# Three layers of modulation vectors, and two parts of the first one's, as dot products along the free axis on VectorE

## The chip, the cores and the metric

One core of one Trainium2 chip. The metric is the device time in microseconds; the kernel before was run 3 times on the chip and executed once more under the profiler. Matmuls are in float32 or float32r.

## The reference

Four diffusion-transformer layers on 256 latent and 256 context tokens of width 1024, followed by a second block (pooling, gated linear attention, a mixture of experts). What the change touches is how each layer's modulation vectors are made:

```python
silu_c, silu_cc = silu(c), silu(c_ctx)                 # two vectors of 1024
for i in range(4):
    sh_a, sc_a, g_a, sh_m, sc_m, g_m = split(silu_c @ mod_w[i] + mod_b[i], 6)   # mod_w[i]: 1024 x 6144
    # the same with silu_cc for the context stream where it is still used
    h = rms_norm(x, norm_mix_g[i]) * (1 + sc_a) + sh_a
    x = x + g_a * mixer(h)          # Fourier, differential attention, latent attention, Fourier
    h = rms_norm(x, norm_mlp_g[i]) * (1 + sc_m) + sh_m
    x = x + g_m * square(relu(h @ w1)) @ w2
```

So `mod_w` is 4 matrices of 25 MB, each multiplied with one or two vectors.

## The kernel before

Activations lie feature-major: feature `128*m + p` of tile `m` on partition `p`, tokens along the free axis, latent (columns 0 to 255) beside context. Every weight matrix is read in panels of 1024 rows by 128 columns. A panel is split into two float32r parts: ScalarE copies `w_hi` (`split_hi`), VectorE subtracts to get `w_lo` (`split_lo_at`), and TensorE makes three products per 128 rows (`split_product`). There is a ring of 4 split panels, and a panel is split 3 ahead of its use (`AHEAD`). An MLP is 4 blocks; a block is 16 steps `j`, one panel each: 8 of the first matrix (then relu and square), 8 of the second (then `add_gated`, which needs the gate vector). The order on each engine is written out by hand; SyncE issues all loads of 1 MB units in one queue, and waits in it for the buffer of each.

The modulation vectors are made in two ways:

- Layer 0: 24 units (`mod_unit`) of 128 rows by 2048 columns, 8 for each third of the 6144 columns. A unit is 4 float32 matmuls side by side in the array, with the two silu vectors as the weights' columns (32 wide, zero padded). ScalarE copies the sum to SBUF, `turn_first` transposes it, and `first_read` on VectorE adds the bias. The last third (shift, scale and gate; the scale is its middle part) is made while the Fourier mixer's last projection runs: units 0 and 1 behind panel 1, 2 and 3 behind panel 2, then one behind each of the panels 3 to 6; its transposes stand behind panel 7.
- Layers 1 to 3: 96 loads of 128 rows by 1536 columns. VectorE multiplies each with the scalar of its partition and adds it to `mod_acc` (`mod_fold`), inside the MLPs of the layers 0 to 2. After 8 loads `sum_mod` adds over the partitions with 8 matmuls on TensorE (`mod_acc` against a column of ones), ScalarE copies, `turn_mod` transposes, and `mod_read` copies to `mod`. There are 9 such groups, 4 in `mlp0`, 4 in `mlp1`, 1 in `mlp2`.

Between two stages of the first layer (`boundary`), the projection's panels 4 to 7 are made for the latent half first and then for the context half (`half_outputs`), so that the norm of the latent half can start early. In it TensorE stands at `half_sum` (the sum of squares over the partitions, behind 4 of the 8 products of the first context tile) until VectorE has added the square of the last latent tile (`add_square`).

Of the kernel before, what the change touches and what calls it, by code (L numbers as in the profile page):

```python
# [380 lines left out]
MOD_RING = 4  # L381
MOD_COLS = 6 * D // BLOCKS
MOD_UNITS = KT
MOD_PART = MOD_COLS // 4
MOD_STEPS = [1, 2, 4, 5, 7, 8, 10, 11]
MOD_SUM_AT = 13
FIRST_GROUPS = 3
FIRST_COLS = 6 * D // FIRST_GROUPS
FIRST_PART = FIRST_COLS // 4
FIRST_RING = 3  # L390
FIRST_UNITS = FIRST_GROUPS * MOD_UNITS
ROWS_AFTER = {1: range(0, 3), 2: range(3, 6), 3: range(6, 9), 4: range(9, 12), 5: range(12, 14), 6: range(14, 16)}
SCALED_AHEAD = [("scale", 0), ("scale", 1), ("sum", 0), ("scale", 2), ("sum", 1), ("scale", 3), ("sum", 2), ("sum", 3)]
THIRD_GROUP_AT = {1: [0, 1], 2: [2, 3], 3: [4], 4: [5], 5: [6], 6: [7]}


MOD_TO = {}
MOD_FOLDS = {}


def place_mods():


    n = 0
    for b in range(BLOCKS):
        MOD_TO[FIRST_GROUPS + b] = [(1, b, 0, 2)]
        MOD_FOLDS[0, b] = [(MOD_STEPS[u], n + u, 1, b, u, (0, 1)) for u in range(MOD_UNITS)]
        n += MOD_UNITS
    for b in range(2):
        MOD_TO[FIRST_GROUPS + BLOCKS + b] = [(2, b, 0, 2)]  # L410
        MOD_FOLDS[1, b] = [(MOD_STEPS[u], n + u, 2, b, u, (0, 1)) for u in range(MOD_UNITS)]
        n += MOD_UNITS
    for b in range(2, BLOCKS):
        MOD_TO[FIRST_GROUPS + BLOCKS + b] = [(2, b, 0, 1), (3, b - 2, 1, 1)]
        MOD_FOLDS[1, b] = [(MOD_STEPS[u], n + 2 * u + i, 2 + i, b - 2 * i, u, (i,))
                           for u in range(MOD_UNITS) for i in range(2)]
        n += 2 * MOD_UNITS
    MOD_TO[FIRST_GROUPS + 2 * BLOCKS] = [(3, 2, 0, 1), (3, 3, 1, 1)]
    for b in range(BLOCKS):
        MOD_FOLDS[2, b] = [((1, 4, 8, 11)[q], n + q, 3, 2 + q % 2, 2 * b + q // 2, (q % 2,)) for q in range(4)]  # L420
        n += 4
    MOD_FOLDS.update({(3, b): [] for b in range(BLOCKS)})


place_mods()
MOD_READ = {(1, 0): 5, (1, 1): 7, (2, 0): 9, (2, 1): 11, (3, 0): 11, (3, 1): 12}


def mod_group(layer, b):


    if layer == 2:
        return FIRST_GROUPS + 2 * BLOCKS if isinstance(b, int) and b == BLOCKS - 1 else None
    return FIRST_GROUPS + BLOCKS * layer + b if layer < 2 and isinstance(b, int) else None
# [3 lines left out]
def build_program(nc, a, out):  # L438
# [8 lines left out]
    with ctx:  # L447
# [46 lines left out]
        pick = sb("pick", [P, 2, 32])  # L494
# [4 lines left out]
        mod_raw = [sb(f"mod_raw{r}", [P, MOD_COLS]) for r in range(MOD_RING)]  # L499
        mod_rows = sb("mod_rows", [P, MOD_PART], over=at["vec_rows"])  # L500
        first_raw = [sb(f"first_raw{r}", [P, FIRST_COLS], over=work + r * 4 * FIRST_COLS) for r in range(FIRST_RING)]
        assert FIRST_RING * FIRST_COLS <= MOD_RING * MOD_COLS
        mod_acc = sb("mod_acc", [P, 2, MOD_COLS])
# [5 lines left out]
        base = at["mod_acc"]  # L509
# [8 lines left out]
        first_rows = sb("first_rows", [P, FIRST_PART])  # L518
        assert base <= at["mod_acc"] + 2 * MOD_COLS * 4, base
# [96 lines left out]
        assert base <= at["mod_acc"] + 2 * MOD_COLS * 4, base  # L616
# [46 lines left out]
        mod_ps = psum[4]  # L663
        pv_ps = psum[4]
# [48 lines left out]
        mod_w = a["mod_w"].rearrange("l (k p) (b c) -> l b k p c", p=P, b=BLOCKS)  # L713
        first_w = a["mod_w"][0].rearrange("(k p) (b c) -> b k p c", p=P, b=FIRST_GROUPS)
# [25 lines left out]
        def _(sp):  # L740
# [21 lines left out]
            def load_mod(n, layer, block, u, i=None):  # L762

                freed = n - MOD_RING + 1
                if freed > 0 or i is not None:
                    sp.wait_ge(s("mod_folded"), later(freed, i, MOD_UNITS))
                else:
                    sp.wait_ge(s("first_used"), FIRST_UNITS)
                sp.dma_start(mod_raw[n % MOD_RING][:, :], mod_w[layer, block, u]).then_inc(s(f"mod_in{n % MOD_RING}"), 16)

            def load_mlp(layer, region_free=None):
# [8 lines left out]
                def mods(n, b):  # L780
                    _, n, of, block, u, _ = MOD_FOLDS[layer, b][n]
                    load_mod(n, of, block, u)

                def block(b, text):
                    for x in text.split():
                        what, n = x[0], int(x[1:])
                        if what == "w":
                            weights(n, b)
                        elif isinstance(b, int):
                            mods(n, b)  # L790
                        else:
                            load_mod(n, 1, b, n, b)

                eight = "w0 m0 m1 w1 m2 w2 m3 w3 w4 w5 m4 m5 w6 m6 w7 m7"
                sixteen = "w0 m0 m1 w1 w2 m2 m3 w3 w4 w5 m4 m5 w6 m6 m7 w7 m8 m9 m10 m11 m12 m13 m14 m15"
                if layer == 0:
                    block(0, eight)
                    with sp.Fori(1, BLOCKS) as b:
                        block(b, eight)
                elif layer == 1:  # L800
                    block(0, "w0 w1 w2 w3")
                    region_free()
                    block(0, "m0 m1 m2 m3 w4 w5 m4 m5 w6 m6 w7 m7")
                    block(1, eight)
                    block(2, sixteen)
                    block(3, sixteen)
                elif layer == 2:
                    block(0, "w0 w1 w2 w3")
                    region_free()
                    block(0, "m0 m1 m2 m3 w4 w5 w6 w7")  # L810
                    for b in range(1, BLOCKS):
                        block(b, "m0 m1 w0 m2 w1 w2 m3 w3 w4 w5 w6 w7")
                else:
                    with sp.Fori(0, BLOCKS) as b:
                        block(b, "w0 w1 w2 w3 w4 w5 w6 w7")

            mod_b = a["mod_b"].rearrange("l (r c) -> (l r) c", c=P)
# [13 lines left out]
            def load_first(units):  # L831
                for n in units:
                    if n >= FIRST_RING:
                        sp.wait_ge(s("first_used"), n - FIRST_RING + 1)
                    sp.dma_start(first_raw[n % FIRST_RING][:, :],
                                 first_w[n // MOD_UNITS, n % MOD_UNITS]).then_inc(s(f"first_in{n % FIRST_RING}"), 16)

# [8 lines left out]
            load_first(range(FIRST_RING, MOD_UNITS - 3))  # L846
# [3 lines left out]
            load_first(range(MOD_UNITS - 3, MOD_UNITS))  # L850
            four_w = a["fourier_w"][0].rearrange("(k p) (u c) -> u p k c", p=P, c=2 * P)
            load_first(range(MOD_UNITS, 2 * MOD_UNITS))
# [5 lines left out]
            load_first(range(2 * MOD_UNITS, FIRST_UNITS))  # L858
# [3 lines left out]
            for h in range(HEADS // 2):  # L862
# [3 lines left out]
                if h == 0:  # L866
                    sp.wait_ge(s("mod_read"), FIRST_GROUPS + BLOCKS)
# [11 lines left out]
            sp.wait_ge(s("mod_read"), FIRST_GROUPS + 2 * BLOCKS)  # L879
# [30 lines left out]
            sp.wait_ge(s("mod_summed"), 2 * BLOCKS + 1)  # L910
# [69 lines left out]
        def _(pool):  # L980
# [5 lines left out]
            pool.memset(pick[:, :, :], 0.0).then_inc(s("pick"), 1)  # L986
            pool.wait_ge(s("pick"), 1)
            for st in range(2):
                pool.memset(pick[:, st, st:st + 1], 1.0).then_inc(s("pick"), 1)
# [47 lines left out]
        def _(act):  # L1037
# [108 lines left out]
            def boundary(n0, x0, name, layer, group=None):  # L1146
# [1699 lines left out]
        def _(dve):  # L2846
# [53 lines left out]
            def boundary(n0, t0, x0, name, layer, gate, before=0, group=None):  # L2900
# [32 lines left out]
                if group:  # L2933
                    mod_read(group, MOD_TO[group])
# [1110 lines left out]
```

## Time and profile before

| | |
|---|---|
| runs | 2028.79, 2032.46, 2033.71 us (median 2032.46) |
| the profiled execution | span 2028.9 us; the page gives no other time of it |
| granted TensorE clock, mean | 0.984 |
| TensorE busy | 96% |
| VectorE busy | 73% |
| ScalarE busy | 50% |
| DMA | 343.51 MB, mean 169 GB/s |

The span is from the first to the last instruction. In the page's lines "L1842" is a line of the kernel, "out<-in" are buffers with their numbers left out, and "x" counts instructions. Matmuls overlap, so the distance between two starts says what one costs, and not its duration.

### The profile page before, as it was taken

What the parts mean: (1) busy time and instruction counts of PE and PEld (TensorE: products, weight loads), DVE (VectorE), ACT (ScalarE), POOL (GpSimd) and SP (SyncE); (2) the same over time, 40 slices, a digit from 0 to 9 for tenths busy, and PEclk for the clock granted to TensorE, in tenths of its full rate; (3) what the DMA queues carried; (4) which work ended last, traced back from release to release, by engine and by line L of the source; (5) the groups of instructions that cost most, each with busy time, mean ns of one, the idle gap of its engine ahead of it and who ended that gap; (6) DMA issues with size and microseconds to landing.
All of it is one profiled execution on the core that took longest, in us unless ns stands there. A gap on an engine that the chain in (4) does not pass through costs nothing.

```text
span 2028.9 us, 31376 instructions
## 1 busy us (share of the span) xinstructions
PE 1947.6 (96%) x11840; PEld 1693.3 (83%) x11840; DVE 1479.8 (73%) x2298; ACT 1023.4 (50%) x1730; POOL 21.7 (1%) x43
## 2 busy tenths in 40 slices
PE   6999999999999999999999787999999999999998
PEld 4688888889787888888888667999999999997886
DVE  3569576687667758685858588788887667776796
ACT  5353323235666656232333577555555456655685
POOL 0200000000000000000000100000000000000000
PEclk9999999999999999999999899999999999999999
DMA  7866464541211234545765311577645555417795
GB/s 288 326 206 211 139 211 136 169 158 48 84 63 63 68 119 132 193 151 167 263 237 166 83 54 46 188 259 265 217 125 182 187 165 168 131 60 232 261 355 196
DMA packets 257044, 343.51 MB, mean 169 GB/s; under 512 B 24487, under 2 KB 235266, under 8 KB 253842
## 3 DMA queue, kind: packets, MB, share of 16 engines
q1 hardware_dynamic: 256914, 341.74, 50.7%
q8 instruction: 85, 1.39, 0.3%
q14 instruction: 45, 0.37, 0.1%
HBM read 340.67 MB, written 1.05 MB: 168 GB/s over the span
## 4 chain that ended last, share of the span: by engine, by line
PE 79%; DVE 8%; ACT 6%; issue 4%; DMA 1%; SPq 0%; DVEq 0%; ACTq 0%
PE bank L1842 24%; PE bank L1843 23%; PE bank L1844 23%; PE bank L2694 2%; PE bank L2684 1%; ACT p_raw L1396 1%; DVE w_lo L2849 1%; ACT p_raw L1384 1%; DVE p_all L3358 1%; PE bank L1894 1%; ACT w_hi L1048 1%; PE bank L1913 1%; ACT mp_raw L1564 1%; ACT norm L1141 1%; DVE neg_max L3367 1%
## 5 line engine op out<-in xcount | busy, mean ns | idle before, releaser
L2849 DVE TENSOR_TENSOR w_lo<-w_raw,w_hi 128x1024 fp32r<-128x1024 f32 x449 | 546.0, 1222 | 60.6 <-ACT w_hi L1048 31.6
L1048 ACT ACTIVATE w_hi<-w_raw 128x1024 fp32r<-128x1024 f32 x350 | 368.0, 1053 | 387.6 <-PE bank L1844 379.2
L1842 PE MATMUL bank<-h_hi,w_hi 128*128 128x512 f32 (+3 forms) x1360 | 467.2, 344 | 10.2 <-DVE h_lo L2886 6.0
L1843 PE MATMUL bank<-h_lo,w_hi 128*128 128x512 f32 (+3 forms) x1360 | 460.3, 338 | 0.0
L1844 PE MATMUL bank<-h_hi,w_lo 128*128 128x512 f32 (+3 forms) x1360 | 459.7, 338 | 0.0
L1842 PE MATMUL bank<-g_hi,w_hi 128*128 128x256 f32 (+1 forms) x1216 | 404.0, 332 | 6.8 <-DVE g_lo L3412 3.6
L1843 PE MATMUL bank<-g_lo,w_hi 128*128 128x256 f32 (+1 forms) x1216 | 400.0, 329 | 0.0
L1844 PE MATMUL bank<-g_hi,w_lo 128*128 128x256 f32 (+1 forms) x1216 | 399.8, 329 | 0.0
L1842 PEld LDWEIGHTS bank<-h_hi,w_hi 128*128 128x128 f32 x1360 | 257.7, 189 | 49.7 <-issue 12.8
L1844 PEld LDWEIGHTS bank<-h_hi,w_lo 128*128 128x128 f32 x1360 | 257.7, 189 | 27.6
L1843 PEld LDWEIGHTS bank<-h_lo,w_hi 128*128 128x128 f32 x1360 | 257.9, 190 | 26.4 <-issue 0.3
L1842 PEld LDWEIGHTS bank<-g_hi,w_hi 128*128 128x128 f32 x1216 | 232.2, 191 | 34.9 <-DVE g_lo L3412 4.5
L1844 PEld LDWEIGHTS bank<-g_hi,w_lo 128*128 128x128 f32 x1216 | 232.1, 191 | 20.5
L1843 PEld LDWEIGHTS bank<-g_lo,w_hi 128*128 128x128 f32 x1216 | 232.3, 191 | 19.4
L3004 DVE SCALAR_TENSOR_TENSOR mod_acc<-mod_raw,silu_c,mod_acc 128x1536 f32<-128x1536 f32 x126 | 224.8, 1812 | 1.5
L3073 DVE SCALAR_TENSOR_TENSOR x<-bank,mod,x 128x256 f32<-128x256 f32 x192 | 87.4, 480 | 114.4 <-PE bank L1844 113.6
L1301 ACT ACTIVATE norm<-bank 128x512 f32<-128x512 f32 x64 | 38.2, 597 | 189.4 <-PE bank L1844 189.4
L3220 DVE TENSOR_TENSOR norm<-norm 128x512 f32<-128x512 f32 (+1 forms) x128 | 70.9, 554 | 72.0 <-ACT norm L1301 67.4
L1739 ACT ACTIVATE w_hi<-w_raw 128x1024 fp32r<-128x1024 f32 x99 | 104.1, 1060 | 35.0 <-PE bank L1844 23.6
L3223 DVE TENSOR_TENSOR g_lo<-norm,g_hi 128x512 fp32r<-128x512 f32 (+1 forms) x128 | 71.6, 559 | 13.3
L1842 PE MATMUL bank<-u_hi,w_hi 128*128 128x258 f32 x256 | 72.9, 285 | 0.0
L1843 PE MATMUL bank<-u_lo,w_hi 128*128 128x258 f32 x256 | 72.4, 283 | 0.0
(539 smaller groups left out, 2805.0 us busy)
## 6 DMA issues: line engine op xcount, KB each, us to landing
w_raw<-in_mlp_w SPq DMA_DIRECT2D x128, 1024.0 KB, 5.6
mod_raw<-in_mod_w SPq DMA_DIRECT2D x96, 768.0 KB, 4.7
first_raw<-in_mod_w SPq DMA_DIRECT2D x24, 1024.0 KB, 5.1
w_raw<-in_w_expert_gate SPq DMA_DIRECT2D x34, 512.0 KB, 4.8
w_raw<-in_w_expert_up SPq DMA_DIRECT2D x34, 512.0 KB, 6.1
w_raw<-in_w_expert_down SPq DMA_DIRECT2D x17, 1024.0 KB, 5.8
w_raw<-in_diff_w_qkv SPq DMA_DIRECT2D x12, 1024.0 KB, 5.1
w_raw<-in_fourier_w SPq DMA_DIRECT2D x8, 1024.0 KB, 7.6
```

What stands on the lines that cost most here:

```text
L1048: act.activation(split_panel(W_hi[n % RING], n), raw_panel(n), ACT.Copy).then_inc(s("w_hi"), 1)
L1301: act.activation(relu[j % 2][:, 0:n_cols], bank[(t0 + j) % BANKS][:, 0:n_cols], ACT.Relu).then_inc(s("relu"), 1)
L1739: act.activation(W_hi[(p0 + n) % RING][:, :], raw_panel(p0 + n), ACT.Copy).then_inc(s("w_hi"), 1)
L1842: pe.matmul(dst, w_hi, r_hi, start=start, stop=False)
L1843: pe.matmul(dst, w_hi, r_lo, start=False, stop=False)
L1844: return pe.matmul(dst, w_lo, r_hi, start=False, stop=stop)
L2694: ins = pe.matmul(slot_out[half][:, :], e[x % 2][:, k, 0:P], v[:, w], start=x % 4 == 0 and k == 0 and q == 0, stop=x % 4 == 3 and k == 1 a ...
L2849: dve.tensor_tensor(split_panel(W_lo[n % RING], n), raw_panel(n), split_panel(W_hi[n % RING], n).bitcast(F32), ALU.subtract).then_inc(s("p ...
L3004: ins = dve.scalar_tensor_tensor(acc, raw, c, acc, ALU.mult, ALU.add)
L3073: ins = dve.scalar_tensor_tensor(X[:, m, c], bank[t % BANKS][:, c], mod[layer][:, gate_at + m, st:st + 1], X[:, m, c], ALU.mult, ALU.add)
L3220: dve.tensor_tensor(squared, relu[j % 2][:, c], relu[j % 2][:, c], ALU.mult).then_inc(s("g_sq"), 1)
L3223: dve.tensor_tensor(G_lo[:, j, c], squared, G_hi[:, j, c].bitcast(F32), ALU.subtract).then_inc(s("g_lo"), 1)
```

## The change

The layer 0 matmuls keep two groups instead of three: shift and scale of the mixer, then its gate and the MLP's scale (2 rows of the 6, in two pieces). Everything else is made as follows. The host hands in `mod_w` transposed as well (`mod_t`, 6144 x 1024 per layer). A unit is now two tiles of 128 output features, each a row of 1024 inputs on its partition, 80 units of 1 MB in a ring of 3. The two silu vectors are spread over all partitions as `c_all`: TensorE transposes them once, they are written to a scratch tensor in HBM (`c_store`), and read back with a broadcast, once before `mlp0`, once in `mlp1` and once in `mlp2`. A fold is then one fused instruction, which multiplies the tile with `c_all`, sums along the free axis, starts from the bias and writes one column of `mod`. There are 240 folds; `MOD_STEPS` gives their places. 16 of them (the shift, 8 tiles for two streams) stand in the `boundary` before `mlp0`: 4 ahead of it and 2, 2, 2, 2, 1, 1, 1, 1 behind its tiles; ScalarE waits for them ahead of the latent half's norm. `pick`, `sum_mod`, `turn_mod`, `mod_read`, the third group of `mod_unit` and the ScalarE copies of these are gone.

```diff
-MOD_RING = 4
+MOD_RING = 3
+MOD_PAIR = 2
-FIRST_GROUPS = 3
+FIRST_GROUPS = 2
...
+    take("first", [(0, 4)])
+    take("four0", enumerate([2, 2, 2, 2, 1, 1, 1, 1]))
+    for b in range(BLOCKS - 1):
+        take(("mlp", 0, b), enumerate([2, 2, 1, 2, 2, 1, 2, 2] + [2] * KT))
+    take(("mlp", 0, BLOCKS - 1), enumerate([2] * KT + [2, 1, 2, 1]))
+    some = [2, 1] * 4
+    for b, counts in enumerate(([0, 0, 1, 1, 1, 1, 2, 2] + some, 2 * some, 2 * some, some + [2, 1, 2, 1, 2])):
+        take(("mlp", 1, b), enumerate(counts))
+    for b in range(BLOCKS - 1):
+        take(("mlp", 2, b), enumerate([0] * KT + [1] * KT))
...
+            def load_mod(n):
+                if n < MOD_RING:
+                    sp.wait_ge(s("first_used"), FIRST_UNITS)
+                else:
+                    sp.wait_ge(s("mod_folded"), sum(x[0] <= n - MOD_RING for x in MOD_OPS))
+                layer, t = MOD_UNITS[n]
+                sp.dma_start(mod_raw[n % MOD_RING][:, :, :],
+                             mod_w[layer, :, t:t + MOD_PAIR, :]).then_inc(s(f"mod_in{n % MOD_RING}"), 16)
+            def spread_c():
+                sp.dma_start(c_all[:, :, :].rearrange("p s c -> p (s c)"),
+                             c_store.rearrange("(o c) -> o c", o=1).to_broadcast([P, 2 * D])).then_inc(s("c_all"), 16)
...
                 root(name, LAT, 0)
+                if name == "mlp0":
+                    act.wait_ge(s("mod_folded"), folds_through(0, 4 * KT - 1))
...
-            def sum_mod(g, i=None):
-                pe.wait_ge(s("mod_read"), later(g, i, 1))
-                folded = {9: 64, 10: 80, 11: 96}.get(g, MOD_UNITS * (g - FIRST_GROUPS + 1))
-                pe.wait_ge(s("mod_folded"), later(folded, i, MOD_UNITS))
-                for row in range(2):
-                    for j in range(4):
-                        ins = pe.matmul(mod_ps[32 * j:32 * (j + 1), 0:MOD_PART], pick[:, row, :],
-                                        mod_acc[:, row, j * MOD_PART:(j + 1) * MOD_PART], start=(row == 0), stop=(row == 1))
...
-                    for u in THIRD_GROUP_AT.get(m, []):
-                        mod_unit(u, 2)
...
+            def mod_folds(stage, j):
+                for n, i, layer, t, st in MOD_STEPS.get((stage, j), []):
+                    dve.wait_ge(s(f"mod_in{n % MOD_RING}"), 16 * (n // MOD_RING + 1))
+                    dve.wait_ge(s("c_all"), 16 * (2 + (stage[1] if stage[0] == "mlp" else 0)))
+                    bias = vcol("mod_b_lo" if layer < 2 else "mod_b_hi", MOD_TILES * (layer % 2) + t)
+                    raw = mod_raw[n % MOD_RING][:, i, :]
+                    again = (n, i, layer, t, 1) in MOD_OPS and st == 0
+                    if again and folds_before(layer, t):
+                        dve.wait_ge(s("mod_folded"), folds_before(layer, t) - 1)
+                    dve.tensor_tensor_reduce(mod_prod[:, :] if again else raw, raw, c_all[:, st, :], 1.0, bias, ALU.mult,
+                                             ALU.add, mod[layer][:, t, st:st + 1]).then_inc(s("mod_folded"), 1)
...
                 first_read(1)
                 dve.wait_ge(s("mod_sum"), 2)
                 add_bias(0, 2)
+                mod_folds("first", 0)
                 boundary(p0, t + 4 * KT + 2, X_AT["four0"], "mlp0", 0, (0, 2 * KT))
```

`first_read` now copies and adds in two pieces and makes the scale in both of its calls (before: one piece, and no scale in the second). The VectorE and SyncE programs of `mlp0` are written out for each block instead of looped.

## Rows read from the trace of the kernel before

**Rows 1.** The page: span, busy time, and the chain that ended last.

```profile
span 2028.9 us, 31376 instructions
...
PE 1947.6 (96%) x11840; PEld 1693.3 (83%) x11840; DVE 1479.8 (73%) x2298; ACT 1023.4 (50%) x1730; POOL 21.7 (1%) x43
...
PE 79%; DVE 8%; ACT 6%; issue 4%; DMA 1%; SPq 0%; DVEq 0%; ACTq 0%
```

**Rows 2.** Busy windows: stretch, PE, PEld, DVE, ACT, POOL, clock, DMA share, GB/s.

```profile
148.00:235.50 87.50, 87.50 (x403) 71.55 (x403) 66.93 (x72) 30.48 (x39) 0.00 (x0) 1.00 0.56 181
...
81.44:119.70 38.26, 38.26 (x246) 27.84 (x245) 19.44 (x45) 8.77 (x14) 0.00 (x0) 1.00 0.64 228
```

**Rows 3.** The same view, a stretch of `mlp2`.

```profile
1360.00:1420.00 60.00, 60.00 (x500) 60.00 (x499) 50.64 (x74) 33.17 (x48) 0.00 (x0) 1.00 0.77 266
```

**Rows 4.** Groups by line, whole span: busy us, mean ns of one, idle before.

```profile
L3004 DVE SCALAR_TENSOR_TENSOR mod_acc<-mod_raw,silu_c,mod_acc 128x1536 f32<-128x1536 f32 x126 | 224.8, 1812 | 1.5
...
L3006 DVE TENSOR_SCALAR mod_acc<-mod_raw,silu_c 128x1536 f32<-128x1536 f32 x18 | 17.6, 1015 | 0.0
...
L1913 PE MATMUL bank<-mod_acc,pick 128*32 128x384 f32 x144 | 13.5, 492 | 0.0
```

**Rows 5.** TensorE's timeline at one group's sum and transposes: start, duration.

```profile
208.94 0.39 PE L1844 MATMUL bank<-g_hi,w_lo 128*128 128x512 f32 x1
209.25 1.50 PE L1913 MATMUL bank<-mod_acc,pick 128*32 128x384 f32 x16
210.68 0.50 PE L1842 MATMUL bank<-g_hi,w_hi 128*128 128x512 f32 x1
...
216.30 0.49 PE L1921 MATMUL bank<-ident,mod_rows 128*128 128x128 f32 x3
216.54 0.48 PE L1842 MATMUL bank<-g_hi,w_hi 128*128 128x512 f32 x1
```

**Rows 6.** TensorE's timeline at units of the third group.

```profile
86.50 0.39 PE L1844 MATMUL bank<-h_hi,w_lo 128*128 128x512 f32 x1
...
86.82 1.92 PE L1894 MATMUL bank<-first_raw,silu_c 128*32 128x512 f32 x16
...
88.67 0.51 PE L1842 MATMUL bank<-h_hi,w_hi 128*128 128x512 f32 x1
...
101.62 0.39 PE L1844 MATMUL bank<-h_hi,w_lo 128*128 128x512 f32 x1
...
102.94 0.39 PE L1842 MATMUL bank<-h_hi,w_hi 128*128 128x256 f32 x1
```

**Rows 7.** VectorE by line, 81.44 to 119.7 us: what ended its idle time.

```profile
L2914 DVE SCALAR_TENSOR_TENSOR x<-bank,mod,x 128x256 f32<-128x256 f32 x12 | 5.4, 480 | 18.5 <-PE bank L1844 18.5
```

**Rows 8.** Timeline: split of panel 3, last square added, TensorE's sum, last latent `h_lo`.

```profile
86.43 1.23 DVE L2849 TENSOR_TENSOR w_lo<-w_raw,w_hi 128x1024 fp32r<-128x1024 f32 x1
...
119.27 0.42 DVE L2869 TENSOR_TENSOR norm<-norm,norm 128x256 f32<-128x256 f32 x1 [0.15 <-ACT norm L1074]
...
119.97 0.60 PE L1954 MATMUL bank<-norm,ones 128*128 128x256 f32 x2
...
136.36 0.43 DVE L2886 TENSOR_TENSOR h_lo<-norm,h_hi 128x256 fp32r<-128x256 f32 x1 [0.52 <-ACT h_hi L1144]
```

**Rows 9.** TensorE alone in two windows: stretch, busy, granted clock, DMA share.

```profile
40.00:45.00 5.00, 1.51 (x12) 0.87 0.88 360
45.00:50.00 5.00, 4.59 (x20) 0.50 0.01 3
```

**Rows 10.** Timelines of VectorE and ScalarE: nearest operations to the new one.

```profile
22.07 2.48 DVE L3308 SCALAR_TENSOR_TENSOR rows_lo<-x_rows,o_inv,rows_hi 128x1024 fp32r<-128x1024 f32 x2 [1.29 <-ACT rows_hi L1371]
...
17.96 0.19 ACT L1360 ACTIVATION_READ_ACCUMULATOR row_squares<-x_rows 128x1 f32 x1
```

**Rows 11.** Loads: a kind with KB and median us to landing; SyncE's timeline.

```profile
mod_raw<-in_mod_w SPq DMA_DIRECT2D x96, 768.0 KB, 4.7
...
70.41 32.99 SPq L835 DMA_DIRECT2D first_raw<-in_mod_w  x8
```

More of the change, by code:

```diff
@@ L425 @@
-place_mods()
[L426 to L434, printed above, removed]
+    tiles = [(0, t) for part in ("shift_m", "gate_m") for t in range(LATER_FIRST[part], LATER_FIRST[part] + KT)]
+    tiles += [(layer, t) for layer in range(1, DEPTH) for t in range(MOD_TILES)]
@@ new lines, in place_mods, with take @@
+    for n in range(0, len(tiles), MOD_PAIR):
+        MOD_UNITS.append(tiles[n])
+        for i, (layer, t) in enumerate(tiles[n:n + MOD_PAIR]):
+            streams = 2 if layer < 2 or layer == 2 and t < 2 * KT else 1
+            MOD_OPS.extend((n // MOD_PAIR, i, layer, t, st) for st in range(streams))
+    at = 0
+    def take(stage, counts):
+        nonlocal at
+        for j, n in counts:
+            MOD_STEPS[stage, j] = MOD_OPS[at:at + n]
+            at += n
+    take("first", [(0, 4)])
@@ L438, in build_program, with folds_before, folds_through @@
+    assert at == len(MOD_OPS), (at, len(MOD_OPS))
+place_mods()
+def folds_before(layer, t):
+    return sum((x[2], x[3]) < (layer, t) for x in MOD_OPS)
+def folds_through(layer, t):
+    return folds_before(layer, t + 1)
 def build_program(nc, a, out):
@@ L857, in _ @@
                 load_unit(PLAN.at["four0"]["unit"] + u, [(whole, four_w[u])])
-            load_first(range(2 * MOD_UNITS, FIRST_UNITS))
+            sp.wait_ge(s("c_all"), 16)
+            spread_c()
+            for n in range(len(LATER_FIRST) * KT // MOD_PAIR // 2):
+                load_mod(next(mod_units))
             load_mlp(0)
@@ L2898, in apply, with boundary, folds @@
                     low_rows(name, KT - 1, c)
-            def boundary(n0, t0, x0, name, layer, gate, before=0, group=None):
+            def boundary(n0, t0, x0, name, layer, gate, before=0):
                 lat, con = slice(0, LAT), slice(LAT, TOK)
+                def folds(m):
+                    return {"mlp0": ("four0", m), "mix1": (("mlp", 0, BLOCKS - 1), KT + m)}.get(name, (None, m))
                 def gated(m, streams):
@@ L2931, in boundary @@
                     add_square(name, LAT, m - 1, 0)
+                    mod_folds(*folds(m))
                 add_square(name, LAT, KT - 1, 0)
-                if group:
-                    mod_read(group, MOD_TO[group])
-                if name == "mlp0":
-                    first_read(2)
                 if name == "mix1":
```

274 lines of the change are left out of this document (91 added, 183 removed).

## The prediction

> **What bounds the kernel now.** I read the page first [rows 1]: TensorE is busy for 96% of the span and holds 79% of the chain that ended last, VectorE 8%. The windows show what this means where the change works [rows 2]: in a block of `mlp0` TensorE never stops (87.50 of 87.50 us, clock 1.00) while VectorE has 66.93 us of work. In such a stretch a microsecond taken from TensorE's queue is a microsecond off the time, and VectorE's work costs nothing until it fills the stretch. So the first question is how much leaves TensorE, the second whether VectorE still fits, stage by stage. The stage where this is in doubt is the boundary before `mlp0`: from 81.44 to 119.70 us VectorE works 19.44 us and is idle for 18.8 [rows 2], almost all of it in waits for TensorE's tiles [rows 7], and that stretch ends in a meeting of the two: VectorE's last square ends at 119.69, TensorE's `half_sum` stands right behind it at 119.97 [rows 8]. The other stretches are seen in the groups by line and in the timelines.
>
> **What leaves TensorE.** Matmuls of a panel start 0.23 us apart. Behind the one at 208.94 the next would start at 209.17; with the sum between them it starts at 210.68, 1.51 later, and is itself 0.11 longer (0.50 for 0.39). The transposes cost 216.54 - 216.30 = 0.24, with 0.09 of the same [rows 5]. That is 1.95 us a group, and there are 9 groups (the 144 records of the sum are 9 times 8 matmuls of two passes each [rows 4]): **-17.6 us**, 8 of the 9 in places where TensorE never waits, the ninth in `mlp2`, which is the same [rows 3]. The third group of layer 0: two units together cost 88.67 - 86.73 = 1.94, one alone 102.94 - 101.85 = 1.09 [rows 6]; two pairs and four single ones are 8.2, with 0.1 behind each of the six and 0.4 for four transposes 9.2 us. These stand in the doubtful stretch.
>
> **What comes to VectorE.** 144 operations on 1536 columns go, 126 of 1.81 us and 18 of 1.01, 242 us in all [rows 4]. 240 fused operations on 1024 columns come. The trace shows none like it. The nearest is a three-operand one on 1024 columns with a pointer scalar: two in 2.48 us, so 1.20 from start to start [rows 10]. The new one also puts out a sum; on ScalarE such a read of the accumulator is 0.19 us [rows 10]. The cost lies between 1.15 (the 1.81 on 1536 columns scaled to 1024 gives 1.21, the last part overlapping) and 1.40 (1.20 plus the whole 0.19); I take **1.25**, near the three-operand row. Then 240 are 300 us, 58 more than before, spread over three MLPs.
>
> The Trainium skill (VectorE: DVE Perf Modes, "Two Vector instructions with no wait between them") says that an operation which also writes out its accumulator is two instructions. It gives no price; if that second one costs what ScalarE's does, the sum is that of the upper end, 1.40.
>
> **Do the MLP blocks hold it?** A block of `mlp0` has 66.93 of 87.50, of which 14 to 16 folds are 27.4; 39.5 is other work. With 30 folds of 1.25 it is 77, so TensorE stays the bound; the point from which VectorE decides is (87.5 - 39.5)/30 = 1.60 us a fold. In `mlp1` 20 to 24 folds of 1.25 stand in for 16 of 1.81: no more work than before. In `mlp2` VectorE has 50.64 of 60 [rows 3]; in a block of 46 us 8 folds (10.0) stand in for 4 (7.2), 90% in all; it fits with little room, and the panels split ahead take up a step that is too long. I cost all three at 0; the cover is VectorE's idle time, and below 1.60 us it lasts.
>
> Loads: a unit is issued when the unit three before it is folded. By the order in the diff, a unit in `mlp0` is issued 4 to 6 steps (22 us and more) before its first fold, in the second half of `mlp1` 2 to 4 steps (11 us and more); a load of 768 KB lands after 4.7 us [rows 11]. The bytes are as before, 24 + 96 x 0.75 = 96 MB against 16 + 80, but for 3 MB of `c_all`. SyncE's queue has the weight units behind each such wait, but their slots become free no earlier. Cost 0; if one is late, VectorE waits for it, and the panels split 3 ahead (16 us) cover that. The small work that goes (ScalarE's ten copies, `mod_read`, the bias additions) and that comes (one transpose and one 8 KB store at the start, while TensorE waits for its first input) lies in idle time: 0.
>
> **The boundary before `mlp0`.** Here 16 folds come, 20.0 us at 1.25, and 0.45 for the second piece and the scale of `first_read`, against 18.8 us idle. So VectorE runs without a gap from 81.44 and ends 1.6 us later than before, and that end, not TensorE, sets `half_sum`. TensorE arrives early: without units it would be at that place about 9 us sooner, some of which it spends waiting for the split panels 3 and 5 to 7 (its split stands at 86.43 now [rows 8]; 0.45 and 4 folds ahead of it move its end to 93.1, and TensorE wants it at 86.73 + 24 x 0.23 = 92.2; the later ones stand behind 2 folds each), the rest, about 4 us, in front of `half_sum`. So all 9.2 us are given back here: **+1.6** instead of -9.2. Second, the wait lowers the clock: TensorE was busy 1.51 of 5 us at 40 to 45, and was granted 0.50 in the 5 us behind it [rows 9], that is 1.2 GHz, half of the 2.4 GHz of 1.00. The same 5 us behind this wait cost 2.4 us of the context half's products, before which nothing can be made up, since the first products of `mlp0` follow directly: **+2.4**. The latent half's chain (root, inverse, `h_lo` until 136.8 [rows 8]) moves with `half_sum` and stays hidden behind this. Last, `first_read` for group 0 stands on the chain before the Fourier products: **+0.35** for the three more small operations of 0.17 to 0.2.
>
> Does the data arrive? The queue reaches the new loads where it issued the third group, from 70.41 [rows 11]. The first unit is the fourth MB behind that, with 2 MB of weights and `c_all` before it: at 360 GB/s [rows 9] it is there at 82, at 228 [rows 2] at 89. Its folds would start at 86.9. The 228 is what was asked for and not what the engines can, so I take no wait; late data is a rival.
>
> **Sum.** -17.6 + 1.6 + 2.4 + 0.35 = -13.2 us, against the span of 2028.9: 2015.7. That span lies 3.6 below the median of the runs; against the median the forecast is **2019 us** (0.993). Its own range: at 1.15 a fold and with no loss of clock -17.2, that is 2015; at 1.40 the boundary costs 2.4 more and its slow stretch may double, -8.4, that is 2024. The three runs before spread over 4.9 us, which makes 2012 to 2026.
>
> **Rivals.**
> - *VectorE at half rate.* If the fused operation with two float32 inputs and a sum takes two cycles where the three-operand rows take one, it is 2.2 us. The point from which this decides is 1.60 us a fold in the first three blocks of `mlp0`. There 30 folds are 66 + 39.5 = 105.5 against 87.5: 18 us each, 54; the boundary 16 x 0.95 = 15; the fourth block and `mlp1` about 14. In all 83 us over the forecast: about 2100 us, slower. For it: the operation is not in the trace. Against it: the operations with two float32 SBUF inputs in the trace take 1.81 for 1536 and 1.20 for 1024 columns, one cycle an element; that they put out no sum is the only difference. Chance 0.12. The Trainium skill (Vector Engine (DVE) Microarchitecture Reference, "Points that are easy to get wrong") says that the three-operand form with two non-bf16 SBUF sources runs at half throughput. For the form without a sum the rows just named disagree with it, and the rows decide; by the rule the time would be the 2100 of this rival.
> - *Late data before `mlp0`.* The first unit or `c_all` (one 8 KB row read 128 times) lands 5 to 10 us after 86.9. VectorE then stands ahead of the split of panel 3, all of the boundary moves with it: 2019 + 5 to 10, so 2024 to 2029. For it: the 228 GB/s of the same stretch. Against it: 360 GB/s 30 us earlier [rows 9]. Chance 0.14.
> - *The sums were hidden.* If TensorE, rid of them, only waits for VectorE more often in `mlp0` and at the boundary before attention, the 17.6 shrink below 6 and the rest is eaten by the boundary: 2029 to 2036, no change. For it: VectorE goes to 88% in `mlp0` (77 of 87.5). Against it: TensorE was continuous there beside lumps of two 1.81 us folds, and single steps are now more even. Chance 0.10.
> - The forecast: 0.64.
>
> **Chances.** 0.3% is 6 us, about what this measurement can tell. Faster than 2026.4: the forecast and most of the late data, 0.75. Within 0.3%: the hidden sums and the rest of the late data, 0.13. Slower: 0.12. The range that leaves out the half-rate case and little else is 2010 to 2031.
>
> **What would show it.** No rows of L1913 and L1921; a third fewer of first_raw matmuls; TensorE continuous in `mlp0`. VectorE without a gap from 81 to 121, TensorE waiting about 4 us ahead of L1954 and a clock near 0.5 behind it; the first relu of `mlp0` about 4 us later than before, and the end of `mlp0` 4 us earlier. Fused operations of 1.25 to 1.45 us duration, 240 of them. It is wrong if these are over 1.6 us, or if TensorE's waits for `w_lo` in the MLPs come to more than a few us.

## The result and the profile after

The changed kernel takes **2014.61 us** (median of 4 runs, 2013.13 to 2017.39), the kernel before 2030.63 beside it: ratio **0.9921**, 95% interval 0.9907 to 0.9935. The forecast was 2019, range 2010 to 2031.

The page of the kernel after, against [rows 1]:

```profile
span 2011.8 us, 31051 instructions
...
PE 1921.9 (96%) x11602; PEld 1684.5 (84%) x11602; DVE 1531.0 (76%) x2619; ACT 1018.4 (51%) x1721; POOL 22.5 (1%) x40
...
PE 75%; DVE 10%; ACT 6%; issue 5%; SPq 1%; DMA 1%; DVEq 0%; ACTq 0%
```

TensorE has 25.7 us less work and still 96% of the span; VectorE has 51 us more, and its share of the chain grew from 8 to 10%. VectorE's groups by line, against [rows 4]:

```profile
L2971 DVE CUSTOM_DVE_ANT_0 mod_raw<-mod_raw,c_all,vec 128x1024 f32<-128x1024 f32 x160 | 203.0, 1278 | 0.0
L2971 DVE CUSTOM_DVE_ANT_0 mod_prod<-mod_raw,c_all,vec 128x1024 f32<-128x1024 f32 x80 | 102.2, 1277 | 0.0
```

These are 240 folds of 1.28 us duration, with no idle time ahead of any. The timeline of VectorE at the boundary before `mlp0` gives their distance, 1.21 us from start to start at the first (1.204 in the mean of all 240):

```profile
82.03 0.26 DVE L2982 COPY mod<-bank 128x16 f32<-128x16 f32 x2 [2.15 <-PE bank L1908]
...
82.91 4.29 DVE L3030 TENSOR_SCALAR x<-x,gated_b 128x256 f32<-128x256 f32 x16
87.24 1.28 DVE L2971 CUSTOM_DVE_ANT_0 mod_prod<-mod_raw,c_all,vec 128x1024 f32<-128x1024 f32 x1
88.45 0.08 DVE L2971 DVE_READ_ACCUMULATOR2_ANT mod<- 128x1 f32 x1
88.45 1.28 DVE L2971 CUSTOM_DVE_ANT_0 mod_raw<-mod_raw,c_all,vec 128x1024 f32<-128x1024 f32 x1
...
120.07 0.42 DVE L2838 TENSOR_TENSOR norm<-norm,norm 128x256 f32<-128x256 f32 x1
121.79 1.75 DVE L2844 RECIPROCAL norm<-norm 128x256 f32<-128x256 f32 x1 [1.30 <-ACT norm L1111]
```

Each fold is followed by a record of 0.08 us that reads the accumulator, at the same instant as the next fold. That it is an instruction of its own agrees with the Trainium skill (VectorE: DVE Perf Modes, "Two Vector instructions with no wait between them"); here it costs nothing beside the next operation: the three-operand row without a sum has the same 1.20 us [rows 10]. From 82.03 to 120.07 VectorE has no wait. TensorE has waits instead, as its own timeline shows (the value in brackets is the wait, and what ended it):

```profile
107.27 0.39 PE L1847 MATMUL bank<-h_hi,w_hi 128*128 128x256 f32 x1 [1.80 <-DVE w_lo L2818]
...
109.89 0.28 PE L1847 MATMUL bank<-h_hi,w_hi 128*128 128x256 f32 x1
110.00 0.28 PE L1848 MATMUL bank<-h_lo,w_hi 128*128 128x256 f32 x1
...
112.21 0.40 PE L1847 MATMUL bank<-h_hi,w_hi 128*128 128x256 f32 x1 [1.80 <-DVE w_lo L2818]
...
114.76 0.41 PE L1847 MATMUL bank<-h_hi,w_hi 128*128 128x256 f32 x1
114.97 0.41 PE L1848 MATMUL bank<-h_lo,w_hi 128*128 128x256 f32 x1
...
120.55 0.70 PE L1941 MATMUL bank<-norm,ones 128*128 128x256 f32 x2 [2.26 <-DVE norm L2838]
```

and in windows of TensorE alone (stretch, busy, granted clock, DMA share, GB/s):

```profile
110.00:114.00 4.00, 2.20 (x13) 0.81 0.14 33
114.00:117.00 3.00, 3.00 (x20) 0.69 1.02 350
117.00:120.00 3.00, 1.29 (x11) 1.00 0.77 307
120.00:125.00 5.00, 4.46 (x35) 1.00 0.01 4
```

The last latent panel (panel 7, from 112.21) is made in part at the lower level of the clock (0.21 us from matmul to matmul at 114.8, 0.12 at 109.9), but TensorE waits for VectorE behind it anyway; behind `half_sum` (120.55) the clock is 1.00.

Where the time went, by landmarks of the two traces (us; a block runs from first relu to first relu):

| stretch | before | after |
|---|---|---|
| start to `first_read` of group 1 | 81.44 | 82.03 |
| from there to `half_sum` | 38.53 | 38.52 |
| to the first relu of `mlp0` | 28.78 | 28.86 |
| block 0 of `mlp0` | 78.99 | 78.96 |
| blocks 1 and 2, each | 89.10 | 87.03 |
| block 3 and attention, to `mlp1` | 377.1 | 375.9 |
| `mlp1`, its blocks 0 / 1 / 2 | 78.99 / 89.10 / 89.10 | 76.91 / 87.04 / 87.04 |
| first relu of block 3 to the first tile of `mlp2` | 266.2 | 263.8 |
| `mlp2` and `mlp3` | 385.5 | 383.4 |
| the rest | 337.0 | 335.3 |

So the time came off where a group left TensorE, about 2.06 us a time, except in block 0 of `mlp0`; and of the 9.2 us of the third group nothing was left. The blocks repeat within 0.02 us from trace to trace; the longer stretches, which hold the groups of both blocks 3 and of `mlp2`, differ by 1.7 to 3.2 us among traces in which they do the same work, so there the 2.06 are read with that doubt. Block 0 has a new wait in TensorE's timeline, behind its eight panels of the first matrix:

```profile
183.79 0.50 PE L1847 MATMUL bank<-g_hi,w_hi 128*128 128x512 f32 x1 [1.71 <-DVE g_lo L3167]
```

### The profile page after: what moved, and what is told of

Read it like the earlier page. It is cut to its first block, busy times and chain, and to the rows that moved or that the text cites. A ratio compares the mean times of both kernels' runs of the same rounds, so it can differ in the third digit from the quotient of the medians.

```text
span 2011.8 us, 31051 instructions
## 1 busy us (share of the span) xinstructions
PE 1921.9 (96%) x11602; PEld 1684.5 (84%) x11602; DVE 1531.0 (76%) x2619; ACT 1018.4 (51%) x1721; POOL 22.5 (1%) x40
## 4 chain that ended last, share of the span: by engine, by line
PE 75%; DVE 10%; ACT 6%; issue 5%; SPq 1%; DMA 1%; DVEq 0%; ACTq 0%
PE bank L1847 23%; PE bank L1848 23%; PE bank L1849 23%; PE bank L2663 2%; DVE w_lo L2818 2%; PE bank L2653 1%; ACT p_raw L1401 1%; ACT p_raw L1389 1%; DVE p_all L3297 1%; ACT norm L1157 1%; ACT w_hi L1064 1%; ACT mp_raw L1569 1%; DVE x L2886 1%; DVE neg_max L3306 1%; DVE norm L2844 1%
## 5 line engine op out<-in xcount | busy, mean ns | idle before, releaser
L1847 PEld LDWEIGHTS bank<-h_hi,w_hi 128*128 128x128 f32 x1360 | 257.9, 190 | 50.5 <-DVE w_lo L2818 10.8
L2971 DVE CUSTOM_DVE_ANT_0 mod_raw<-mod_raw,c_all,vec 128x1024 f32<-128x1024 f32 x160 | 203.0, 1278 | 0.0
L1304 ACT ACTIVATE norm<-bank 128x512 f32<-128x512 f32 x64 | 38.3, 598 | 189.4 <-PE bank L1849 189.4
L1744 ACT ACTIVATE w_hi<-w_raw 128x1024 fp32r<-128x1024 f32 x99 | 104.1, 1059 | 33.8 <-PE bank L1849 22.5
L2971 DVE CUSTOM_DVE_ANT_0 mod_prod<-mod_raw,c_all,vec 128x1024 f32<-128x1024 f32 x80 | 102.2, 1277 | 0.0
```

The source lines that it names most:

```text
L1304: act.activation(relu[j % 2][:, 0:n_cols], bank[(t0 + j) % BANKS][:, 0:n_cols], ACT.Relu).then_inc(s("relu"), 1)
L1744: act.activation(W_hi[(p0 + n) % RING][:, :], raw_panel(p0 + n), ACT.Copy).then_inc(s("w_hi"), 1)
L1847: pe.matmul(dst, w_hi, r_hi, start=start, stop=False)
L2971: dve.tensor_tensor_reduce(mod_prod[:, :] if again else raw, raw, c_all[:, st, :], 1.0, bias, ALU.mult, ALU.add, mod[layer][:, t, st:st + ...
```

## The experiments

All are edits of the changed kernel; "..." in a cut of code stands for lines left out. "Boundary" is the distance from `first_read` of group 1 to `half_sum`, 38.5 us before and after.

**The folds of the boundary made thin.** Do they alone fill it? The 16 folds work on 32 columns and leave out the rest of each sum.

```diff
-dve.tensor_tensor_reduce(mod_prod[:, :] if again else raw, raw, c_all[:, st, :], 1.0, bias, ALU.mult,
+w = slice(0, 32 if stage in ("first", "four0") else D)
+dst = (mod_prod[:, :] if again else raw)[:, w]
+dve.tensor_tensor_reduce(dst, raw[:, w], c_all[:, st, w], 1.0, bias, ALU.mult,
...
```

> The changed kernel, with the 16 folds of the boundary before mlp0 made on 32 columns in place of 1024 (it leaves out most of that sum; all other folds are whole). In the changed kernel VectorE has no gap from 82.0 to 120.1 us, and 16 folds of 1.2 us are 19.3 us of it. Theory (VectorE's folds alone take back what leaves TensorE there): VectorE ends earlier by more than TensorE needs, TensorE becomes the bound again without its third group, half_sum comes 9 us earlier (near 111.5 for 120.55), the first relu of mlp0 near 140.5 for 149.4, and the whole kernel takes about 2006 us for 2014.6. Rival (data: the first unit or c_all, or SyncE's queue, holds the stretch): half_sum stays within 1 us of 120.5 and the time within 2 us of 2014.6. A second rival, that TensorE now waits more and loses clock in it, would show as a granted clock under 0.9 for 10 us or more and a gain of 4 us or less.

Measured: 2005.37 us (2001.62 to 2006.12; ratio 0.9877, 0.9856 to 0.9897). The boundary is 29.33 us, 9.19 less than 38.52; TensorE is busy for 37.95 of the 38 us from 82 to 120 and stands at `half_sum` without a wait, at 109.91 (stretch, busy, granted clock, DMA share, GB/s):

```profile
82.00:120.00 38.00, 37.95 (x256) 1.00 0.73 257
```

The first relu is at 138.87. The theory holds; neither data nor clock holds the stretch. VectorE's timeline also splits a fold's price:

```profile
88.51 0.24 DVE L2973 CUSTOM_DVE_ANT_0 mod_prod<-mod_raw,c_all,vec 128x32 f32<-128x32 f32 x1
88.68 0.08 DVE L2973 DVE_READ_ACCUMULATOR2_ANT mod<- 128x1 f32 x1
88.68 0.25 DVE L2973 CUSTOM_DVE_ANT_0 mod_raw<-mod_raw,c_all,vec 128x32 f32<-128x32 f32 x1
88.86 0.08 DVE L2973 DVE_READ_ACCUMULATOR2_ANT mod<- 128x1 f32 x1
```

Folds of 32 columns are some 0.175 us apart and folds of 1024 are 1.205, which gives 1.04 ns a column and 0.14 us fixed.

**The sums back on TensorE, as idle work.** What is a group worth?

```diff
+def idle_sums():                      # behind panel 13 of each block that had a sum
+    for row in range(2):
+        for j in range(4):
+            pe.matmul(mod_ps[32 * j:32 * (j + 1), 0:384], silu_c[:, row, :],
+                      ones[:, 0:1].to_broadcast([P, 384]), start=(row == 0), stop=(row == 1))
+def idle_turns():                     # behind panel 14
+    for j in range(3):
+        pe.transpose(mod_ps[:, j * P:(j + 1) * P], ident[:, :], ident[:, :])
...
```

> The changed kernel, with 8 matmuls of 384 columns and 3 transposes, whose results nobody reads, put back at the places of the 9 sums on TensorE. Theory (these were a microsecond for a microsecond of the time): each costs 1.95 to 2.06 us in blocks 1 to 3 of mlp0, in the four of mlp1 and in mlp2, 16 us in all; the one of block 0 of mlp0 costs 0 to 0.5, because TensorE stands there at g_lo for 1.7 us anyway. Time 2030 to 2031 us for 2014.6, level with the kernel before. Rival (the gain came from elsewhere, from a VectorE that has no sums to wait for): under 4 us longer, 2014 to 2018.

Measured: 2033.19 us (2031.51 to 2034.45; ratio 1.0006, 0.9995 to 1.0017), level with before and 18.6 more than the changed kernel, which is 9 times 2.06. Blocks 1 and 2 are 89.1 us again. The expectation for block 0 was wrong: it takes 81.02 us, 2.06 more than 78.96. The wait at `g_lo` is still 1.72 us and stands at step 8; the sum comes at step 13, behind it, where no wait is left to absorb it. So in block 0 two things of like size cancel in the change: a sum of 2.06 us that went and a wait that came.

**The third group back on TensorE.** Were the 9.2 us really given back?

```diff
-FIRST_UNITS = FIRST_GROUPS * KT
+FIRST_UNITS = 3 * KT
+THIRD_GROUP_AT = {1: [0, 1], 2: [2, 3], 3: [4], 4: [5], 5: [6], 6: [7]}
...
-    tiles = [(0, t) for part in ("shift_m", "gate_m") for t in range(...)]
-    tiles += [(layer, t) for layer in range(1, DEPTH) for t in range(MOD_TILES)]
+    tiles = [(layer, t) for layer in range(1, DEPTH) for t in range(MOD_TILES)]
...
+                    for u in THIRD_GROUP_AT.get(m, []):
+                        mod_unit(u, 2)
...
```

> The changed kernel, with shift and gate of layer 0's MLP made on TensorE again, as 8 units in the same places as before; the layers 1 to 3 stay folds (208 of them, 14 in the first block of mlp0). Theory (the 9.2 us that left TensorE here were all given back by 16 folds): the first relu of mlp0 comes at 148.4 to 148.8 as before the change (149.4 in the changed kernel), and since block 0 of mlp0 has 14 folds and not 30 TensorE has no wait at its g_lo, so the block's group of 2 us comes off too: 2.5 to 3 us less than the changed kernel, about 2012 us. Rival (the 9.2 us are part of the 16 us gained): 7 to 9 us more, 2022 to 2024.

Measured: 2013.49 us (2011.33 to 2016.85; ratio 0.9912, 0.9891 to 0.9933). The boundary is 38.53 us. With the units TensorE is the one that is full in it (38.0 us of 38), without them VectorE is (38.3 of 38.5), and the two lengths are equal. Block 0 of `mlp0`, with 14 folds in place of 30, takes 76.91 us and has no wait at `g_lo`. The first relu is at 149.8, later than expected, because the trace comes to `first_read` 1.1 us later than that of before, which has nothing to do with the edit (below). The theory holds in both parts; its 2 us of block 0 are seen in the trace and not in the medians, which differ by 1.1 and whose intervals overlap.

**Folds of 1.47 and of 2.29 us in `mlp0`.** Where does VectorE become the bound? One or four multiplications of 192 columns go ahead of every fold there.

```diff
+for _ in range(1 if stage[0] == "mlp" and stage[1] == 0 else 0):      # the second kernel: range(4 if ...
+    i2 = next(extras)
...
+    dve.tensor_tensor(spare[:, i2 % 2 * 192:(i2 % 2 + 1) * 192], c_all[:, 0, 0:192], c_all[:, 1, 0:192], ALU.mult)
 dve.tensor_tensor_reduce(...)
```

> The changed kernel, with a multiplication of 192 columns ahead of every fold in mlp0, which makes a fold there about 1.4 us. The prediction put the point from which VectorE decides at 1.60 us a fold in a block of 30. Theory: blocks 1 and 2 keep their period of 87.0 us; only the first block, where VectorE has no gap after the first relu, gets 1 to 3.5 us longer; the whole 1 to 4 us longer, near 2014.5 of span for 2011.8. Rival (VectorE is the bound all through mlp0): 112 folds times 0.2 us, 20 us and more.

> The changed kernel, with four multiplications of 192 columns ahead of every fold in mlp0 (one of them costs 0.27 us from start to start), which makes a fold there 2.3 us, about what half rate would have made it. The prediction: above 1.60 us a fold VectorE decides; 30 folds of 2.29 and some 38 us of other work are 107 us, so blocks 1 and 2 take 105 to 108 us each for 87.0, block 0 about 104 for 79, and the whole 65 to 85 us more, 2077 to 2097 of span. Rival (TensorE has more slack in its split panels than that, or VectorE's other work shrinks in its gaps): under 40 us more.

Measured, one run each: 2020.88 and 2085.66 us. With 1.47 us a fold blocks 1 and 2 keep 87.04 us, with 2.29 they take 104.84 and 103.32. The span with 1.47 us is 7.3 us longer, where 1 to 4 was expected. The windows of the two kernels over blocks 1 and 2 (PE, PEld, DVE, ACT, POOL, clock, DMA share, GB/s), first the shorter folds:

```profile
235.50:323.00 87.50, 87.50 (x388) 72.45 (x387) 80.31 (x141) 26.31 (x33) 0.00 (x0) 1.00 0.53 183
323.00:410.00 87.00, 87.00 (x385) 72.04 (x384) 79.90 (x140) 25.97 (x32) 0.00 (x0) 1.00 0.56 192
```

```profile
235.50:323.00 87.50, 74.56 (x309) 59.24 (x308) 86.67 (x191) 22.58 (x29) 0.00 (x0) 0.94 0.43 147
323.00:410.00 87.00, 74.57 (x315) 59.65 (x314) 86.16 (x190) 22.97 (x30) 0.00 (x0) 0.94 0.48 166
```

TensorE is full in the first and VectorE in the second. From 104.1 us for 30 folds of 2.29 the other work is 35.4, and by that VectorE would decide from (87.04 - 35.4) / 30 = 1.72 us a fold, where the prediction had 1.60. This is an estimate: only 1.47 and 2.29 us were run. Block 0 is another matter. With 1.47 us a fold it already takes 83.75 us, 4.8 more, beyond the 3.5 expected: the wait at `g_lo` grows from 1.71 to 4.49 us, and behind it the clock falls.

```profile
187.50:190.00 2.50, 2.49 (x7) 0.57 0.72 292
190.00:195.00 5.00, 5.00 (x21) 0.87 0.44 132
```

That is 1.1 + 0.65 = 1.7 us for the clock, and 2.8 for the wait: together 4.5 of the 4.8. (Of the other 2.5 us of span 1.9 lie in attention, which differs by as much between other traces.) With the long folds block 0 takes 93.9 us, 10 less than expected, and block 3 with attention 398.4, 22.5 more than in the changed kernel; the whole, 72 us more of span, is within what was expected.

**The folds of `mlp0` spread otherwise.**

```diff
-take(("mlp", 0, b), enumerate([2, 2, 1, 2, 2, 1, 2, 2] + [2] * KT))
+take(("mlp", 0, b), enumerate(([2] * KT if b else [0, 1, 1, 1, 2, 1, 2, 2]) + [2] * KT))
```

> The changed kernel, with its folds in mlp0 spread otherwise: 0, 1, 1, 1, 2, 1, 2, 2 in the first eight steps of block 0 in place of 2, 2, 1, 2, 2, 1, 2, 2, and 2 in every step of blocks 1 and 2 (26, 32, 32 and 22 folds for 30, 30, 30 and 22). Theory (the first steps of block 0 are the only ones where VectorE falls behind; it ends 1.7 us late at g_lo): the wait at g_lo goes, block 0 takes 76.9 us from first relu to first relu for 79.0, blocks 1 and 2 stay at 87.04; 2.0 us less, 2012.6 us. Rival (32 folds are too many for blocks 1 and 2, or their units come late): TensorE waits there for w_lo and the time is the same or longer.

Measured: 2014.19 us (2010.82 to 2015.23; ratio 0.9911, 0.9894 to 0.9927). Block 0 takes 76.91 us, with no wait at `g_lo`; blocks 1 and 2, with 32 folds each, 87.04. So the stretch does what was expected, 2.05 us, but the median is only 0.4 lower: five runs that spread over 4.4 us don't settle 2.

**The bias additions on ScalarE.**

```diff
 for m in range(4):                    # ScalarE's boundary
     split_hi(n0 + m + AHEAD)
+    if name == "mlp0" and m < 2:
+        act.wait_ge(s("gated_b"), 1)
+        for i in range(4 * m, 4 * m + 4):
+            for st in range(2):
+                c = slice(st * LAT, (st + 1) * LAT)
+                ins = act.activation(X[:, i, c], X[:, i, c], ACT.Identity, bias=gated_b[:, i, st:st + 1])
...
-for m in range(KT):                   # VectorE's additions
+for m in range(KT if layer else 0):
...
```

> The changed kernel, with the 16 additions of the Fourier bias to x moved from VectorE, where they stand ahead of the boundary's first fold (4.3 us), to ScalarE, which is idle for three quarters of that stretch. Theory (VectorE, without a gap from 82.0 to 120.1 us, sets half_sum): half_sum at 116.2 us for 120.55, the first relu of mlp0 4.3 us earlier, 2010.3 us for 2014.6. Rival (TensorE's waits for the split panels and half_sum are set by the splits on ScalarE or by late units): the additions push the splits back and nothing or less than 1 us is gained.

Measured: 2013.32 us (2011.73 to 2013.75; ratio 0.991, 0.9896 to 0.9925). The boundary is 37.28 us, 1.24 less and not 4.3. Neither the theory nor the rival as I put it came true. The first split on ScalarE does stand 4.0 us later (85.68 for 81.66), but VectorE needs it only at 90.38; what took the gain is a new wait in VectorE's timeline, for the data.

```profile
82.26 0.17 DVE L3033 TENSOR_TENSOR gated_b<-mod,vec 128x16 f32<-128x16 f32 x1
85.55 1.29 DVE L2980 CUSTOM_DVE_ANT_0 mod_prod<-mod_raw,c_all,vec 128x1024 f32<-128x1024 f32 x1 [3.12 <-DMA mod_raw<-in_mod_t]
```

The additions' 4.33 us less the wait of 3.12 is the 1.2 that came off. The first fold starts 3.96 us behind `first_read`; in the changed kernel it comes 5.21 behind it. In the changed kernel's own trace the unit (issued at 74.44, landed 10.8 us later) is there at 85.2, 2.0 us ahead of its fold at 87.24. So the late data of the prediction's rival was 1 to 2 us from being seen.

**Both edits, and then the unit earlier in the queue.**

```diff
+            sp.wait_ge(s("c_all"), 16)
+            spread_c()
+            load_mod(next(mod_units))
             for u in range(2, 4):
                 load_unit(PLAN.at["four0"]["unit"] + u, [(whole, four_w[u])])
-            sp.wait_ge(s("c_all"), 16)
-            spread_c()
-            for n in range(len(LATER_FIRST) * KT // MOD_PAIR // 2):
+            for n in range(len(LATER_FIRST) * KT // MOD_PAIR // 2 - 1):
```

> Both of the last two edits. Theory: they act in stretches one behind the other, so they add: 6.3 us less than the changed kernel, 2008.3 us, and 22 us less than before (ratio 0.989). Rival: an earlier start of mlp0 meets late units or weights in its first block, and less than 5 us remain.

> The kernel with both edits (the other spread in mlp0, the bias additions on ScalarE), and in SyncE's queue c_all and the first unit issued ahead of the last two units of the projection's weights. With the bias additions gone from VectorE its first fold waited 3.1 us for the unit, which landed at 85.5 us, so they gave back 1.7 us and not 4.3. Theory (the first unit is late because 2 MB are ahead of it in engines that are full to 85 us): it lands before 82.5, the first fold has no wait, half_sum comes near 116.5 for 120.0, and the whole takes 2.5 to 3.5 us less than with both edits: 2007.5 to 2008.5 us. Rival (the load waits for the buffers that it shares with layer 0's units, or the weights issued behind it are late for panels 4 and 5): less than 1 us, or slower.

Measured for both edits: 2011.0 us (2008.47 to 2013.22; ratio 0.9899, 0.9881 to 0.9918); boundary 37.31, block 0 76.90: the parts add, at the size that each had alone in the traces (1.2 and 2.05 us), so the whole is 3.6 us less than the changed kernel and not 6.3. With the early unit: **2009.45 us** (2007.35 to 2010.63; ratio 0.9894, 0.988 to 0.9908). The first fold starts at 81.22 with no wait and the boundary is 34.18 us, 4.34 less than in the changed kernel, so all of the additions' time. The median is 1.55 us below that of both edits, where 2.5 to 3.5 was expected, and the two intervals overlap: that this last edit is worth something is seen in the stretches of the trace alone. From `half_sum` to the first relu it is 30.02 us and not 28.86, and the timeline and the windows of TensorE show why:

```profile
114.53 1.22 PE L1949 MATMUL bank<-norm,ones 128*128 128x256 f32 x2 [3.76 <-DVE norm L2846]
115.20 0.78 PE L1855 MATMUL bank<-h_hi,w_hi 128*128 128x256 f32 x1
115.77 0.42 PE L1856 MATMUL bank<-h_lo,w_hi 128*128 128x256 f32 x1
```

```profile
110.00:114.50 4.50, 0.78 (x7) 1.00 0.75 289
114.50:117.00 2.50, 2.47 (x9) 0.50 0.02 7
117.00:120.00 3.00, 3.00 (x24) 0.85 0.00 0
```

Now TensorE has a wait of 0.89 us and one of 3.76 in front of `half_sum`, in place of 1.80, 1.80 and 2.26, and the clock behind it is 0.50, that is 1.2 GHz. The lower clock costs 1.7 us (half of 2.5 and 0.15 of 3), of which some comes back at TensorE's next wait (0.46 us for `h_lo` at 136.34, where the changed kernel has 0.81 at 141.19). So 1.16 of the 4.34 us are given back. It is still the fastest kernel here that leaves nothing out.

**The changed kernel again.**

> The changed kernel once more, beside the run with the early units, so that the two are measured against the same runs of the kernel before. Theory (each stretch goes as its trace shows): 2014.5 us within 1.5, and a trace whose blocks of mlp0 and mlp1 have the periods seen before (79.0 and 87.04 us) within 0.1. The stretch of attention between mlp0 and mlp1, 375.2 to 377.8 us in the traces so far whatever was changed, should differ again by up to 2 us; that would show what of the small differences between runs is not the change's.

Measured beside the last one: 2014.97 us (2013.15 to 2019.40; ratio 0.9925, 0.9911 to 0.994). This interval and that of the early units (to 0.9908) don't meet. Its trace has the same boundary (38.51) and blocks (78.96, 87.04), and block 3 with attention takes 375.86, the same as in the first trace, where I expected a difference; in all other traces but that of the 2.29 us folds it takes 375.1 to 377.8. It comes to block 3 of `mlp1` 0.3 us earlier than the first trace, and its span is 4.1 us longer. Most of that arises before `mlp2` (its first tile at 1295.8 for 1293.1), where TensorE meets the same waits at other clocks. Here is the first trace at the norm behind `mlp1`, then this one:

```profile
1113.22 1.05 PE L1916 MATMUL bank<-ones,norm 128*128 128x1 f32 x8 [2.37 <-DVE norm L2838]
1114.84 1.16 PE L1922 MATMUL bank<-ident,col_rstd 128*128 128x128 f32 x8 [0.57 <-DVE col_rstd L2957]
```

```profile
1112.92 1.87 PE L1916 MATMUL bank<-ones,norm 128*128 128x1 f32 x8 [2.36 <-DVE norm L2838]
1115.36 2.08 PE L1922 MATMUL bank<-ident,col_rstd 128*128 128x128 f32 x8 [0.56 <-DVE col_rstd L2957]
```

## Why the prediction was right, and where it was not

- **What leaves TensorE (-17.6): right, a little small.** A group is 2.06 us and not 1.95 (blocks of 89.10 to 87.04; put back, nine of them cost 18.6). The forecast counted only the first matmul behind the sum and behind the transposes as wider (0.11 and 0.09); in the trace of before the eleven distances behind the sum are together 0.17 us wider than the usual 0.227 each, and the eight behind the transposes 0.12, which makes 2.04 of the 2.06.
- **"I cost all three at 0", for the MLP blocks: wrong for block 0 of `mlp0`, by 2.05 us.** The argument took a block as a whole, 30 folds in 87.5 us. But in block 0 the products of the first three panels lie ahead of the first relu. TensorE then has only five panels, 27.2 us, before it turns to the second matrix. VectorE has to make all eight `g` tiles in that time and a little more; it has no gap of more than 0.11 us from 150.04 to 183.66, with 12 folds among them (a step of two folds takes 4.95 us, 178.71 to 183.66). The last `g_lo` is late, TensorE waits 1.71 us, and the block's group is used up. With the 12 folds ahead of that point cut to 8 the group's gain comes back (76.91 us). For blocks 1 and 2 the step was right (87.04 us, TensorE never waits, VectorE busy for 72.3 of 87.0 us); the point from which VectorE decides there comes out at 1.72 us as an estimate, forecast 1.60.
- **The price of a fold: 1.205 us, forecast 1.25.** The three-operand row [rows 10] was the right neighbour. What half rate would have done is seen in the run with 2.29 us a fold in `mlp0`: 14.9, 17.8 and 16.3 us more in its first three blocks, 49 in all where the rival put 54, and 71 us in the whole, with the folds of the boundary and of `mlp1` left as they are. The prediction took the Trainium skill's rule on two non-bf16 SBUF sources (Vector Engine (DVE) Microarchitecture Reference, "Points that are easy to get wrong") as half of one column per cycle, 2.2 us a fold. So read, it doesn't hold for this operation: a column costs 1.04 ns. But the Trainium skill doesn't say there of what rate the half is. In before the one-source multiplication of 1536 float32 columns takes 1.01 us and the three-operand one 1.81 [rows 4]; against that one-source form two sources do run at nearly half the rate. So these runs refute the prediction's reading of the rule, and not the rule.
- **The third group's 9.2 us, all given back: right, and the step checked from both sides.** Thin folds bring the boundary to 29.33 us, 9.20 below before's 38.53; putting the units back leaves it where it was. The +1.6 on top was not there (38.52): 0.7 of it is the fold's price, and 0.2 the small operations of `first_read` (0.88 us in all for 0.66, forecast 0.45 more). Some 0.5 are the ends of operations: the last 0.08 us of one lie under the next where that follows at once, but stood free, and counted as busy in the 19.44 us, ahead of each of the seven waits of before.
- **The clock behind `half_sum` (+2.4): wrong.** It stood on one wait of 4 us in front of `half_sum`, and the first relu should have come 4 us later than before; it comes 0.66 later (149.41 for 148.75). TensorE's surplus came in five pieces (0.41, 0.40, 1.80, 1.80, 2.26), since the splits of the panels 6 and 7 stand behind two folds each; the slow stretch fell on panel 7, where 1.6 us of it only shortened the next wait. From `half_sum` to the first relu it is 28.86 for 28.78. The kernel with the early unit has the case that was forecast: one wait of 3.76, a clock of 0.50 behind it, and a loss of 1.16 us, half of what I put.
- **+0.35 for the small operations of `first_read`:** not settled. The two traces differ by 0.59 there, and all twelve lie between 80.35 and 83.19.
- **Data:** no wait, as forecast, but by 2.0 us in the changed kernel's trace; the argument from GB/s couldn't have told that from a late unit, so this was partly luck.

The sum by measured parts: -18.5 for nine groups, +2.05 for block 0, 0.0 for the boundary, +0.1 behind it, +0.6 at the start: -15.8, and the medians differ by 16.0. The spans differ by 17.1; the further 1.3 are +0.8 in attention, -0.3 ahead of `mlp2` and -1.7 behind `mlp3`; between the two traces of the changed kernel the last two of these differ by 3.0 and 1.3, so they are not put down to the change. The forecast's -13.2 was 2.6 off in sum because +1.6 and +2.4 that did not come stood against +2.05 that was not foreseen; so in part the sum was right by luck. The rest of the way from 2019 to 2014.6 is the reference: before was at 2032.46 when the forecast was made and at 2030.63 beside the changed kernel. The rival that the sums were hidden is refuted by the run that puts them back; its mechanism, VectorE that comes too late in `mlp0`, was real in one block, the first.

## What to carry to other kernels

Work moved from a full engine to another pays where the full one need not wait for the receiver inside the stretch; count the receiver's load from meeting to meeting and not over the block, for the first block after a start above all. What a stretch gives back when its bound changes is best found by making the moved work thin and then by putting it back: these two runs give both engines' own times. When the bound of a stretch is taken away, the next one may be a microsecond behind (here 1.2 us to the data, and then the clock), so an edit is priced by the distance to the next bound and not by its own length.

## What was not expected of the hardware

- The same waits of TensorE (2.36 and 0.56 us) in two traces of one kernel go with different clocks: 8 small matmuls take 1.05 us in one and 1.87 in the other. From block 3 of `mlp1` to `mlp2` the two traces differ by 3.0 us. That the clock explains much of the spread of some 4 us between runs of one kernel is a guess; it was not tested.
- Behind TensorE's waits of 1.80 us at 107.3 the clock stayed at 1.00, and behind that of 2.26 too; behind the second 1.80 (112.2) it was lower for 3.6 us, behind 3.76 and 4.49 it was 0.50 and 0.57 in the next 2.5 us.
- The fused multiplication with a sum of 1024 float32 columns costs 1.205 us, the same as the three-operand form without a sum; the read of its accumulator (0.08 us) lies beside the next instruction.
